# Dilated value slabs and the last down-projection with 512 moving columns, folded sums, and reordered starts and ends, in a three-layer fp32 block on one core

## The chip, the core and the metric

The kernel runs on one core of a Trainium2 chip (trn2). The metric is the device time of one execution in microseconds (us). The core has five instruction streams: PE (matmuls; the profile lists its weight loads apart as PEld), DVE, ACT, POOL (element-wise engines) and SP, which here only issues DMA transfers. They run side by side and meet at semaphores.

## The reference, cut to what matters

Sequence 256, width 1024, everything fp32. A first block has two layers (an even mixer and an odd mixer, each followed by a squared-ReLU MLP) and ends in an RMS norm; a second block has one layer and ends in another.

```python
def first_block(x, ...):                     # x: 1 x 256 x 1024
    for layer in range(2):
        xn = rms_norm(x, norm_mix[layer])
        x = x + (even_mixer if layer == 0 else odd_mixer)(xn, ...)
        x = x + sq_relu_mlp(rms_norm(x, norm_mlp[layer]), w1[layer], w2[layer])
    return rms_norm(x, norm_final)

def odd_mixer(xn, w_in, w_o, cos, sin):      # three dilation groups, 16 heads of 64
    hcat = (xn @ w_in).reshape(b, s, 3, 3, 16, 64)
    q, k = rope(hcat[:, :, :, 0]), rope(hcat[:, :, :, 1])
    v = hcat[:, :, :, 2]
    return dilated_attention(q, k, v) @ w_o

def second_block(x, mem, ...):
    h = rms_norm(x, mix_norm_gain)
    # one projection feeds a linear recurrence, block attention, attention over mem, and gates
    x = x + (sum_of_gated_branches) @ w_out
    h = rms_norm(x, ffn_norm_gain)
    g = causal_dwconv(h @ w_ffn_gate)
    x = x + (gelu(g) * (h @ w_ffn_up)) @ w_ffn_down     # 3072 -> 1024
    return rms_norm(x, final_norm_gain)
```

## The kernel before, in words

**Weights in slabs.** All weights stream from memory in 192 slabs of up to 128 x 2048 values, in the order that `weight_plan` writes out by hand. SP loads slab n into one of five buffers (`raw`). ACT rounds it to a high part (`whi`, one of three buffers, L975), DVE or POOL subtracts to get the low part (`wlo`, L1357 on DVE, L2020 on POOL). `ahead(n)` on each engine prepares slab n+2. A product (`product`, L515) takes three matmuls for each 128 x 128 weight block: high by high, high by low, low by high. The activations are kept feature by row (`XT`, with `XH` and `XL` as its two parts), so that usually the weight block is stationary and 256 tokens move. `tokens` turns this round: 128 tokens are stationary and 256 weight columns move; the dilated values use it.

**Norms.** Squares of `XT` are added up chunk by chunk into `acc(slot)`, 128 x 512 (`add_square`, on DVE or POOL). `sums` then multiplies with ones on PE to add over the partitions: two plain fp32 matmuls of 256 columns, one for each half of `acc`, and where `cols` is set four more of one column. The profile lists each plain fp32 matmul as two.

**Attention.** Units of work run through a software pipeline over steps s. On PE, `attend(first, n, s)` issues the scores of unit s (L648), the transposes of unit s-2 (L656) and the values of unit s-3 (L685). DVE takes maxima (L1425, L1431) and normalises (L1440), ACT does the exponentials (L1037) and copies the transposed probabilities (L1046), or DVE does (L1448). Other work is put between the steps by hand. In the even layer this is among others the memory input: PE transposes it into four banks (`turn_in`, L587), and DVE's `memory_low` (L1623) is what frees a bank. In the odd layer there are 36 slabs of q, k and v: 10 ahead of the first step, the other 26 beside steps 0 to 23. Each q or k slab (24 in all) goes through a rotation: ACT copies it (L1191) and issues four DMAs that swap halves (L1195), POOL multiplies (L2083), DVE adds (`rotate`, L1696). The four values slabs of a head group use `tokens`.

**Second block.** Gates and branches are blended by DVE (L1895, L1897), ACT makes the high part of the merged rows (L1271) and DVE the low part (L1901). Then follow the output projection `OUT2`, the gated feed-forward (`FF`, 24 slabs) and the last down-projection (`FD`, 12 slabs). Its result stays feature by row; squares, gain, transposes back (L940), sums (L958) and the last scaling come behind it.

## Time and profile before

| | |
|---|---|
| median of 3 runs | 1265.96 us (1265.52 to 1267.0) |
| the profiled execution | 1267.13 us, span 1265.3 us |
| PE busy | 1245.1 us, 98% |
| DVE, ACT, POOL busy | 820.8, 618.7, 274.8 us |
| mean granted PE clock | 0.994 |
| DMA | 214 MB, 169 GB/s |

The span goes from the first to the last instruction; the 1.8 us beside it lie outside of what the profile shows. Busy time of PE contains the pipeline latency of a matmul, so rates are better read from long runs of matmuls in the chain than from the mean duration.

### The profile page before, as it was taken

What the parts mean: (1) busy time and instruction counts of PE and PEld (TensorE: products, weight loads), DVE (VectorE), ACT (ScalarE), POOL (GpSimd) and SP (SyncE); (2) the same over time, 40 slices, a digit from 0 to 9 for tenths busy, and PEclk for the clock granted to TensorE, in tenths of its full rate; (3) what the DMA queues carried; (4) which work ended last, traced back from release to release, by engine and by line L of the source; (5) the groups of instructions that cost most, each with busy time, mean ns of one, the idle gap of its engine ahead of it and who ended that gap; (6) DMA issues with size and microseconds to landing.
All of it is one profiled execution on the core that took longest, in us unless ns stands there. A gap on an engine that the chain in (4) does not pass through costs nothing.

```text
span 1265.3 us, 23972 instructions
## 1 busy us (share of the span) xinstructions
PE 1245.1 (98%) x10309; PEld 1207.0 (95%) x10309; DVE 820.8 (65%) x1106; ACT 618.7 (49%) x765; POOL 274.8 (22%) x205
## 2 busy tenths in 40 slices
PE   7999999999999999999999999999999999999997
PEld 7968899999999999999999999999999999999997
DVE  6768666655565666666877655487876477665653
ACT  5565455544344454545555553345665445444441
POOL 2500010000021202020310000389211595444000
PEclk9999999999999999999999999999999999999998
DMA  9543356555576655464355655555553455555550
GB/s 262 185 134 101 106 170 191 177 189 176 191 225 204 188 170 181 150 191 151 101 166 171 196 171 195 170 172 173 170 165 134 163 170 168 187 180 188 179 167 34
DMA packets 194711, 214.00 MB, mean 169 GB/s; under 512 B 5235, under 2 KB 182718, under 8 KB 194606
## 3 DMA queue, kind: packets, MB, share of 16 engines
q1 hardware_dynamic: 189518, 204.93, 50.3%
q10 hardware_dynamic: 4896, 7.08, 2.0%
q8 instruction: 81, 1.33, 0.5%
q0 software_dynamic: 192, 0.46, 0.1%
q14 instruction: 24, 0.20, 0.1%
HBM read 205.11 MB, written 1.05 MB: 163 GB/s over the span
## 4 chain that ended last, share of the span: by engine, by line
PE 92%; DVE 3%; ACT 2%; POOL 1%; DMA 1%; issue 1%; ACTq 0%; SPq 0%; DVEq 0%; POOLq 0%
PE ps L515 79%; PE ps L648 3%; PE ps L551 3%; PE ps L685 2%; PE ps L656 2%; DVE wlo L1357 1%; PE ps L572 1%; PE ps L535 1%; DVE XL L1391 1%; POOL wlo L2020 1%; DMA TB<-TA 0%; ACT whi L975 0%; ACT SN L1037 0%; ACT XH L1007 0%; ACTq L1195 0%
## 5 line engine op out<-in xcount | busy, mean ns | idle before, releaser
L1357 DVE TENSOR_TENSOR wlo<-raw,whi 128x2048 fp32r<-128x2048 f32 (+1 forms) x155 | 360.1, 2326 | 202.1 <-ACT whi L975 202.0
L515 PE MATMUL ps<-XH,whi 128*128 128x256 f32 x1592 | 451.8, 285 | 0.0
L515 PE MATMUL ps<-XH,wlo 128*128 128x256 f32 x1592 | 448.3, 283 | 0.3 <-DVE wlo L1357 0.3
L515 PE MATMUL ps<-XL,whi 128*128 128x256 f32 x1592 | 448.0, 283 | 0.0
L975 ACT ACTIVATE whi<-raw 128x2048 fp32r<-128x2048 f32 (+1 forms) x189 | 359.5, 1905 | 176.6 <-PE ps L515 154.7
L515 PEld LDWEIGHTS ps<-XH,whi 128*128 128x128 f32 x1592 | 304.3, 192 | 3.2 <-issue 2.9
L515 PEld LDWEIGHTS ps<-XH,wlo 128*128 128x128 f32 x1592 | 304.3, 192 | 0.9 <-DVE wlo L1357 0.8
L515 PEld LDWEIGHTS ps<-XL,whi 128*128 128x128 f32 x1592 | 304.3, 192 | 0.0
L2020 POOL TENSOR_TENSOR wlo<-raw,whi 128x512 fp32r<-128x512 f32 x136 | 180.3, 1358 | 319.5 <-ACT whi L975 319.5
L515 PE MATMUL ps<-HH,whi 128*128 128x256 f32 x832 | 229.5, 283 | 0.0
L515 PE MATMUL ps<-HL,whi 128*128 128x256 f32 x832 | 229.3, 283 | 0.0
L515 PE MATMUL ps<-HH,wlo 128*128 128x256 f32 x800 | 226.5, 283 | 1.0 <-POOL wlo L2020 1.0
L515 PEld LDWEIGHTS ps<-HH,whi 128*128 128x128 f32 x832 | 157.5, 192 | 0.0
L515 PEld LDWEIGHTS ps<-HL,whi 128*128 128x128 f32 x832 | 157.5, 192 | 0.0
L515 PEld LDWEIGHTS ps<-HH,wlo 128*128 128x128 f32 x800 | 153.6, 192 | 1.2 <-POOL wlo L2020 1.2
L2083 POOL TENSOR_TENSOR TB<-TB,BIG 128x512 f32<-128x512 f32 x24 | 42.7, 1781 | 367.4 <-DMA TB<-TA 367.4
L1037 ACT ACTIVATE SN<-SN,stat 128x512 f32<-128x512 f32 (+2 forms) x64 | 38.2, 597 | 102.2 <-DVE stat L1425 93.2
L515 PE MATMUL ps<-whi,XH 128*128 128x256 f32 x256 | 73.2, 286 | 0.0
L515 PE MATMUL ps<-whi,XL 128*128 128x256 f32 x256 | 72.4, 283 | 0.0
L515 PE MATMUL ps<-wlo,XH 128*128 128x256 f32 x256 | 72.4, 283 | 0.0
L515 PE MATMUL ps<-OH,whi 128*128 128x256 f32 x192 | 56.3, 293 | 0.0
L1079 ACT ACTIVATE HH<-TB 128x512 fp32r<-128x512 f32 x32 | 20.2, 632 | 72.7 <-DVE TB L1513 72.7
(229 smaller groups left out, 1604.0 us busy)
## 6 DMA issues: line engine op xcount, KB each, us to landing
raw<-in_mlp_w_dram SPq DMA_DIRECT2D x64, 1024.0 KB, 5.4
raw<-in_od_w_in_dram SPq DMA_DIRECT2D x36, 1024.0 KB, 5.4
raw<-in_w_in_dram SPq DMA_DIRECT2D x24, 1024.0 KB, 5.2
raw<-in_w_ffn_gate_dram SPq DMA_DIRECT2D x12, 1024.0 KB, 5.1
raw<-in_w_ffn_up_dram SPq DMA_DIRECT2D x12, 1024.0 KB, 5.1
raw<-in_w_ffn_down_dram SPq DMA_DIRECT2D x12, 1024.0 KB, 5.0
raw<-in_ev_w_in_dram SPq DMA_DIRECT2D x6, 1024.0 KB, 11.6
TB<-TA ACTq DMA_DIRECT2D x96, 64.0 KB, 4.1
```

What stands on the lines that cost most here:

```text
L515: m = pe.matmul(to, l[c][a], r[c][b], start=first and k == 0, stop=last and k == 3 * n - 1)
L535: i = pe.matmul(b[:, m * S:m * S + S], w[m][c][a], x[c][z], start=k == 0, stop=k == len(order) - 1)
L551: i = pe.matmul(b[n][:, m * S:m * S + S], h[a], x[c][z], start=m == c == a == z == 0, stop=m == 1 and c == 7 and z == 1)
L648: m = pe.matmul(banks[u][:, lo:hi], l, r, start=start, stop=stop)
L656: m = pe.transpose(b[:, to:to + P], SN[:, u % 3, of:of + P], ident[:, :])
L685: m = pe.matmul(b[p0:p0 + n, a:z], v, PT[:, u % 3, lo:hi], start=start, stop=stop)
L975: act.activation(whi_of(n), raw_of(n), ACT.Copy, scale=1.0).then_inc(*tell(s_whi, ("whi", n)))
L1037: m = act.activation(SN[:, u % 3, lo:hi], src[:, lo:hi], ACT.Exp, bias=stat[:, u % 3, k:k + 1], scale=-1.0 if biased else 1.0, accum_out=s ...
L1079: act.activation(HH[:, 512 * j:512 * j + 512], TB[j % 2][:, :], ACT.Copy, scale=1.0).then_inc(*tell(s_xhi, ("hhi", layer, j)))
L1357: dve.tensor_tensor(wlo_of(n), raw_of(n), f32(whi_of(n)), ALU.subtract).then_inc(*tell(s_wlo, ("wlo", n)))
L2020: m = pool.tensor_tensor(lo[:, v], r[:, v], f32(hi[:, v]), ALU.subtract)
L2083: pool.tensor_tensor(z, z, twice(RP[:, S:512]), ALU.mult).then_inc(*tell(s_pool, ("sine", k)))
```

## The change

Seven edits in one.

1. The dilated values come in slabs of 4 k-chunks by 512 columns (eight heads), two slabs to a product of 128 tokens by 512 columns. They have half as many matmuls, of 512 columns each. The order of the 36 slabs is the list `DILATED`; 14 stand ahead of the first step and one beside each of steps 0 to 21. The first three output slabs (`pieces`) go one block to each of steps 22 to 33.
2. The last down-projection makes rows instead of features: 128 tokens stationary, 512 weight columns moving. `XT` is transposed to rows during the feed-forward (`rows_in`). Squares, mean and scaling are done on rows; the last gain is loaded spread over all partitions.
3. `sums` gets one folded half: the engine that adds the squares adds the two halves of `acc` too.
4. On PE the values of unit s-3 are issued ahead of the transposes of unit s-2. On DVE `memory_low` is issued ahead of the outputs of the step.
5. In the blend ACT prepares the branch slabs' successors ahead of the high parts of the merged rows.
6. The identity and first gains are loaded from ACT's queue, ahead of which nothing stands, and ACT does one small activation early (its table is loaded then).
7. `keep_busy` puts 12 matmuls of ones between the first transposes.

```diff
-    for hb in range(4):
-        for g, n in ORDER:
-            add("odd", wo, 0, 8, ((3 * g + n) * 16 + 4 * hb) * 64, 256)
+    for kind, b, g, k in DILATED:
+        if kind == "qk":
+            add("odd", wo, 0, 8, ((3 * g + k) * 16 + 4 * b) * 64, 256)
+        else:
+            add("odd", wo, 4 * k * P, 4, ((3 * g + 2) * 16 + 8 * b) * 64, 512)
...
-    down("fd", A["w_ffn_down_2"][0], 24)
+    for half in range(2):
+        for k in range(6):
+            add("fd", A["w_ffn_down_2"][0], 4 * k * P, 4, 512 * half, 512)
...
+    return qk(0) + v(0) + qk(1) + qk(2) + v(1) + qk(3)
...
+EARLY = 14
...
+        pieces = {22 + 4 * k + j: [(k, j)] for k in range(3) for j in range(4)}
...
-            def sums(name, slot, n=2, cols=False, dilated=False):
+            def sums(name, slot, n=1, cols=False, dilated=False):
...
+                if 0 <= s - 3 < n and members(group_of(first + s - 3))[-1] == first + s - 3:
+                    values(group_of(first + s - 3))
                 if 0 <= s - 2 < n:
                     transposes(first + s - 2)
-                if 0 <= s - 3 < n and members(group_of(first + s - 3))[-1] == first + s - 3:
-                    values(group_of(first + s - 3))
...
+            keep_busy(3)
             b = bank(("mixgain",))
...
+            keep_busy(4)
             for c2 in range(4):
+                if c2 == 2:
+                    keep_busy(2)
                 turn_in(("x", c2), [xrow[:, t, :] for t in range(2)], ("x", c2 // 2), c2)
+            keep_busy(3)
...
+                    for t in range(2):
+                        if k == 0:
+                            bank(("odd v", hb, g, t))
+                        b = ps[bank_of.get(("odd v", hb, g, t), 0)]
...
+                        product(b[:, :], xt, w_ready(n, 4, 0, 512), event, first=k == 0, last=k == 1)
...
+                if EARLY + s < len(DILATED):
+                    odd_slab(EARLY + s)
...
+            for q in range(2):
+                b = [bank(("down", 2, q, t)) for t in range(2)]
+                for k in range(6):
...
+                        product(b[t][:, :], ht, w_ready(n, 4, 0, 512), event, first=k == 0, last=k == 5)
...
-            b = bank(("last",))
-            once.wait_ge(*at(("norm", "n7")))
...
-            rows_out(3)
...
                 if s == 14:
+                    ahead(BLENDS + BLEND.index(("branch", 4)))
+                    ahead(BLENDS + BLEND.index(("branch", 5)))
                     branch(4)
                     branch(5)
...
+            for t in range(2):
+                squared_rows(1, t)
+                row_root(t)
+                scaled_row(t, 1)
+            once.wait_ge(*at(("row", 1, 1)))
+            act.dma_start(out[0, P:2 * P, 512:1024], YR[:, 1, 512:1024]).then_inc(*tell(s_out, ("out", 1), by=16))
...
+                if done:
+                    a = acc(slot)
+                    once.wait_ge(*at(("summed", norm, i)))
+                    dve.tensor_tensor(a[:, 0:S], a[:, 0:S], a[:, S:2 * S], ALU.add).then_inc(*tell(s_sum, ("norm", norm)))
...
-                attend(EVEN, 16, s)
+                attend(EVEN, 16, s, lambda: memory_low(s - 6) if 6 <= s < 10 else None)
...
+            for t in range(2):
+                row_sums(1, t)
+                row_mean(t)
+                row_scale(t)
```

On DVE, at steps 6 and 7 of the even layer, the instructions stand so before; OL is the low part of an attention output, HL that of the memory input (L1623 is `memory_low`).

```order
L1425 ISA SN,stat<-ps0,BIG 128x256
L1425 ISA stat 128x1
L1458 TENSOR_TENSOR OL<-ps2,OH 128x256
L1623 SCALAR_TENSOR_TENSOR HL<-ps6,V,HL 128x256 x2
L1437 RECIPROCAL stat<-stat 128x2
L1440 TENSOR_SCALAR SN<-SN,stat 128x256 x2
```

And so after, where L1669 is `memory_low` and L1504 the output:

```order
L1471 ISA SN,stat<-ps0,BIG 128x256
L1471 ISA stat 128x1
L1669 SCALAR_TENSOR_TENSOR HL<-ps6,V,HL 128x256 x2
L1504 TENSOR_TENSOR OL<-ps1,OH 128x256
L1483 RECIPROCAL stat<-stat 128x2
L1486 TENSOR_SCALAR SN<-SN,stat 128x256 x2
```

The instruction that frees bank 6 has moved in front of the output, which waits for ACT.

On ACT, at the end of the blend, before (whi<-raw prepares a weight slab; HH<-BIG is the high part of merged rows):

```order
L1277 ACTIVATE BIG<-BIG 128x2048
L1055 ACTIVATE OH<-ps0 128x256
L975 ACTIVATE whi0<-raw2 128x2048
L1271 ACTIVATE HH<-BIG 128x512 x2
L975 ACTIVATE whi1<-raw3 128x2048
L1271 ACTIVATE HH<-BIG 128x512 x2
L975 ACTIVATE whi2<-raw4 128x2048
```

And after:

```order
L1303 ACTIVATE BIG<-BIG 128x2048
L1082 ACTIVATE OH<-ps0 128x256
L1002 ACTIVATE whi0<-raw2 128x2048
L1002 ACTIVATE whi1<-raw3 128x2048
L1297 ACTIVATE HH<-BIG 128x512 x4
L1002 ACTIVATE whi2<-raw4 128x2048
```

The second output slab (raw3) no longer stands behind the first two merged pieces.

On PE, the end of the program before:

```order
L515 MATMUL ps3<-HH,wlo1 128x256
L515 MATMUL ps3<-HL,whi0 128x256
L940 MATMUL ps4<-ident,BIG 128x128 x4
L958 MATMUL ps5<-ones,SQ 128x1 x4
L940 MATMUL ps6<-ident,BIG 128x128 x4
```

And after:

```order
L535 MATMUL ps1<-wlo1,HH 128x512
L535 MATMUL ps1<-whi0,HH 128x512
L535 MATMUL ps1<-whi0,HL 128x512
L535 MATMUL ps1<-wlo1,HH 128x512
L294 UNCONDITIONAL_BRANCH
```

Nothing is left for PE behind the last product.

## Rows read from the trace of the kernel before

**Rows 1.** The page: busy us, share of the span, instructions.

```profile
PE 1245.1 (98%) x10309; PEld 1207.0 (95%) x10309; DVE 820.8 (65%) x1106; ACT 618.7 (49%) x765; POOL 274.8 (22%) x205
```

**Rows 2.** Whom PE waited for: us in total, times, longest.

```profile
PE ps L587 <- DMA BIG<-in_x_dram: 2.5, 2, 2.1
PE ps L648 <- DVE HL L1623: 2.2, 1, 2.2
PE ps L958 <- DVE SQ L1367: 2.1, 1, 2.1
...
PE ps L515 <- POOL wlo L2020: 1.0, 1, 1.0
```

**Rows 3.** Chain that ended last, by time: start us, us, what.

```profile
24.43 0.86 PE ps L572 x4
25.30 0.79 PE ps L576 x8
...
80.96 1.72 PE ps L791 x4
...
1219.39 17.27 PE ps L515 x144
```

**Rows 4.** Chain in the even layer, from 88 us.

```profile
89.44 4.46 PE ps L648 x16
93.89 1.04 PE ps L656 x4
94.94 1.82 PE ps L685 x8
...
103.53 2.53 PE ps L648 x16
106.06 0.59 PE ps L656 x4
106.65 1.01 PE ps L685 x8
```

**Rows 5.** Timeline of DVE there; in brackets its idle time before.

```profile
88.17 0.42 DVE L1458 TENSOR_TENSOR OL<-ps,OH 128x256 fp32r<-128x256 f32 x1 [2.21 <-ACT OH L1055]
...
90.75 0.68 DVE L1448 COPY PT<-ps 128x512 f32<-128x512 f32 x1
```

**Rows 6.** Windows: busy (instructions) of PE, PEld, DVE, ACT, POOL; PEclk; DMA, GB/s.

```profile
89.70:96.50 6.80, 6.80 (x28) 3.03 (x26) 4.58 (x13) 2.67 (x10) 0.00 (x0) 0.50 0.01 2
...
600.00:624.00 24.00, 24.00 (x238) 21.57 (x233) 21.72 (x55) 16.09 (x32) 10.60 (x8) 1.00 0.29 89
```

**Rows 7.** Timeline: the start, and POOL at the end of the blend.

```profile
1.63 1.84 SPq L2152 DMA_DIRECT2D BIG<-in_x_dram  x4
...
7.14 1.28 ACT L1007 ACT_TABLE_LOAD   x1 [7.14 <-DVE XT L1543]
...
23.02 2.29 DVE L1357 TENSOR_TENSOR wlo<-raw,whi 128x2048 fp32r<-128x2048 f32 x1 [1.18 <-ACT whi L975]
...
1020.84 21.85 POOL L2020 TENSOR_TENSOR wlo<-raw,whi 128x512 fp32r<-128x512 f32 x16 [3.16 <-ACT whi L975]
```

**Rows 8.** Chain through the rotation of one slab.

```profile
416.18 0.61 ACTq L1195
...
417.46 5.64 DMA TB<-TA
...
423.16 2.82 POOL TB L2083
```

**Rows 9.** Timeline of the tail.

```profile
1254.40 0.42 DVE L1493 TENSOR_TENSOR TA<-ps,RS 128x256 f32<-128x256 f32 x1 [2.00 <-PE ps L515]
...
1256.04 0.69 DVE L1367 TENSOR_TENSOR SQ<-SQ 128x512 f32<-128x512 f32 x1 [0.75 <-ACT SQ L991]
...
1260.02 0.71 ACT L1347 ACTIVATE BIG<-BIG,RS 128x512 f32<-128x512 f32 x1
...
1260.76 1.82 SPq L2182 DMA_DIRECT2D out_dram<-BIG  x4
```

More of the change, by code:

```diff
@@ L724, in mlp, with keep_busy @@
                 down(layer, W2[layer], h_ready(layer, 32))
+            def keep_busy(n):
+                once.wait_ge(*at("ones"))
+                for _ in range(n):
+                    pe.matmul(ps[7][:, 0:P], ones[:, :], ones[:, :], start=True, stop=True)
+            keep_busy(3)
             b = bank(("mixgain",))
@@ L930, in tensor, with rows_in @@
             features_by_chunks([FF], x)
-            features(FF + 1, x, between=lambda: sums("n6", 0))
+            features(FF + 1, x, between=lambda: sums("n6", 0, cols=True))
+            def rows_in(j):
+                b = bank(("rows", j))
+                for t in range(2):
+                    for c in range(2):
+                        m = pe.transpose(b[:, t * S + c * P:t * S + c * P + P], XT[:, 2 * j + c, t * P:(t + 1) * P], ident[:, :])
+                m.then_inc(*tell(s_product, ("product", "rows", j)))
@@ L1318, in scalar @@
                 if j == 0:
-                    root("n6", 0)
+                    root("n6", 0, cols=True)
                 else:
@@ L1322, in scalar @@
                 ahead(FF + 2 * j + 1)
+                if j in (3, 5, 7, 9):
+                    i = (j - 3) // 2
+                    b = take(("rows", i))
+                    act.activation(XR[:, :, 256 * i:256 * i + 256], pair(b[:, :]), ACT.Copy, scale=1.0).then_inc(
+                        *tell(s_act_out, ("taken", "rows", i)))
                 once.wait_ge(*at(("ffn conv", j)))
@@ L1325, in scalar @@
             ffn_high(11)
-            def rows_out(j):
-                b = take(("rows", j))
-                act.activation(orow[:, :, 256 * j:256 * j + 256], pair(b[:, :]), ACT.Copy, scale=1.0).then_inc(
-                    *tell(s_act_out, ("taken", "rows", j)))
-            for j in range(4):
-                for s in range(3):
-                    ahead(FD + 3 * j + s)
-                once.wait_ge(*at(("xt", "down", 2, j)))
-                if j == 0:
-                    once.wait_ge(*at("ones"))
-                    act.activation(GG[:, 0:1], ones[:, 0:1], ACT.Sqrt)
-                square("n7", 1, j, x0[j], ("xt", "down", 2, j))
-                if j:
-                    rows_out(j - 1)
@@ L1342, in scalar, with squared_rows @@
[L1342 to L1347 removed]
+            def squared_rows(q, t):
+                once.wait_ge(*at(("xr", q, t)))
+                act.activation(SQ[:, 2 * q + t, :] if q + t < 2 else SN[:, 2, :], XR[:, t, 512 * q:512 * q + 512], ACT.Square, accum_out=stat[:, t, q:q + 1]).then_inc(
+                    *tell(s_square, ("rows squared", q, t)))
@@ new lines, in row_root, with scaled_row @@
+            def row_root(t):
+                once.wait_ge(*at(("mean", "n7", t)))
+                act.activation(r7[:, t:t + 1], r7[:, t:t + 1], ACT.Sqrt).then_inc(*tell(s_root, ("sqrt", "n7", t)))
+            def scaled_row(t, q):
+                once.wait_ge(*at(("root", "n7", t)))
+                once.wait_ge(*at(("yr", q, t)))
+                v = YR[:, t, 512 * q:512 * q + 512]
+                act.activation(v, v, ACT.Copy, scale=r7[:, t:t + 1]).then_inc(*tell(s_act, ("row", t, q)))
@@ L1988, in vector @@
             ffn_low(11)
-            for j in range(4):
-                down(2, FD, 3, r6, j)
-                if j:
-                    add_square("n7", 1, j, j == 3)
-                for c in (2 * j, 2 * j + 1):
-                    m = dve.tensor_scalar(XG[:, c, :], XT[:, c, :], gain("fin2", c), None, ALU.mult)
-                m.then_inc(*tell(s_dve, ("gained", j)))
-            b = take(("last",))
-            r7 = RS[:, 1, 0:2]
-            dve.tensor_scalar(r7, b[:, 0:2], 1.0 / D, EPS, ALU.mult, ALU.add).then_inc(
-                *tell(s_dve_out, ("mean", "n7"), ("taken", "last")))
@@ new lines, in vector @@
+            for k in range(6):
+                ahead(FD + k)
+            for t in range(2):
+                row_sums(0, t)
+            for t in range(2):
+                once.wait_ge(*at(("rows squared", 0, t)))
+                m = dve.tensor_scalar(stat[:, t, 2:3], stat[:, t, 0:1], 1.0 / D, EPS, ALU.mult, ALU.add)
+            m.then_inc(*tell(s_dve, "rows' first half"))
+            for k in range(6, 12):
+                ahead(FD + k)
+            once.wait_ge(*at("rows' first half"))
```

242 lines of the change are left out of this document (119 added, 123 removed).

## The prediction

> **What bounds the kernel now.** I read four views, in this order. The page first: PE is busy for 1245.1 of 1265.3 us, no other engine for more than 65% [rows 1]. That busy share holds pipeline latency, so the next view is the list of PE's waits: few of its entries reach 1 us: the start (2.5), the even layer (2.2), the tail (2.1) and the blend (1.0) [rows 2]. Everywhere else PE goes from one product into the next. The chain of what ended last shows the pace: 144 matmuls in 17.27 us, 119.9 ns each [rows 3]. Last come the windows, where one stretch of the even layer runs at a granted clock of 0.50, 1.2 GHz, while the other one is at 1.00, 2.4 GHz [rows 6]. So three things shorten this kernel: less matmul time, the few waits, and the tail behind the last product. Work taken off another engine counts only where one of these waits hangs on it.
>
> **512 moving columns.** The dilated values had 12 slabs of 48 matmuls, 576 in all, and the last down-projection had 12 x 48 too. Both become half as many, of 512 columns: 1152 matmuls of 256 turn into 576 of 512. One of 256 costs 119.9 ns [rows 3]. At 2.4 GHz and one column a cycle, 256 columns take 106.7 ns, so 13.2 ns are something else. What is it? No fp32r matmul of 512 columns is in the trace. Plain fp32 ones are, at two cycles a column: of 256 columns 215 ns (0.86 over 4), where the columns take 213.3, and of 512 columns 430 ns (1.72 over 4), where they take 426.7 [rows 3]. Their remainder is 2 to 3 ns. With a single moving column one still costs 99 ns (0.79 over 8) [rows 3]: that is about what loading a 128 x 128 weight block takes. So where the columns last 213 ns the load hides, and where they last 107 ns it nearly fills the time. I read the 13.2 ns as the load that does not quite hide. With 512 columns it would have 213 ns to hide in, and a matmul would cost 213.3 + 2.5 = 215.8, say 216 ns. The saving is 2 x 119.9 - 216 = 23.8 ns, times 576 = 13.7 us. The bounds: if the 13.2 ns are paid once by each matmul whatever its length, it costs 226.5 ns and the saving is 7.7 us; if the pace goes with the columns alone (0.468 ns a column), nothing is saved. A loss would need a remainder above 26 ns, twice that of 256 columns. I take 13.7, since plain fp32 is the nearest row and its remainder did not grow.
>
> The Trainium skill ("TensorE: Matmul & The Clock Gate", section "Back-to-back issue gap") has the isolated gap as N/2.4 + 2.5 ns, 109.2 at 256 columns and 215.8 at 512. The trace disagrees at 256 (119.9 ns), so by that formula alone, at both ends, the edit would be worth 1.5 us, and with the measured 256 it would be worth 13.8.
>
> **Folded sums.** Eight of the ten `sums` lose one plain matmul of 256 columns, two instructions of 215 ns, 0.43 us each and 3.4 together. Five with `cols` also lose four instructions of 99 ns, 0.39 us each and 2.0 together; n6 gets as many new ones, 0.4. Net 5.0 us, all of it PE time between products. The fold is one more 256-wide addition, on DVE about half of 0.69 us [rows 9], on POOL half to all of 1.37 (21.85 over 16) [rows 7]. PE's waits name no `sums` except the last, L958 [rows 2], so it stays covered by the products ahead; uncovered it would cost 0.4 to 1.4 us at one norm.
>
> **Even layer.** PE stands 2.2 us before the scores at 89.44 [rows 2], because `memory_low` frees the bank only behind the output at 88.17, for which DVE itself stood idle for 2.21 us waiting for ACT [rows 5]. `memory_low` now goes into that idle time and PE starts at 87.24. What is late next is the values, now ahead of the transposes: they want the copy that DVE makes at 90.75 for 0.68 us [rows 5], which moves up by the 0.85 that `memory_low` takes behind the output (88.59 to 89.44) [rows 4, 5], to end near 90.6. PE's scores end at 87.24 + 2.53 = 89.8 [rows 4], so 0.8 us of the wait come back: 1.4 gained. The second part is the clock. It fell at 89.70, just behind the 2.2 us of idleness, and stayed for 6.8 us [rows 6]. In it scores, transposes and values took 4.46 + 1.04 + 1.82 = 7.32 us; the same at full clock take 2.53 + 0.59 + 1.01 = 4.13 [rows 4]. That is 3.2 more, if the clock stays up. I take 4.6 in all, and for the lower end that the clock falls all the same: then the values and transposes still take 2.86, PE is through at 87.24 + 2.53 + 0.8 + 2.86 = 93.4 instead of 96.8, and the slow time left until 96.5 costs half of itself, 1.5, on what follows: 1.8. Nothing is added above 4.6.
>
> **Blend.** PE waits 1.0 us for POOL's low part of the second output slab [rows 2]. POOL had been idle for 3.16 us until ACT's high part came [rows 7], which stood behind two merged pieces. Now it goes first. The merged pieces come later by one preparation of a slab, and PE wants the first of them only behind branch 5. I take 1.0 and bound it by 0 and 1.3. Steps 13 and 14 gain nothing else, as PE runs through them.
>
> **Start.** The table load of 1.28 us stood between the first `XT` and everything that followed [rows 7], and x is asked for at 1.63, behind two small loads that take some 0.9 us to issue [rows 7]. Both leave the path: 2.2 us at most until PE's first product. From there to the third slab DVE's low part decides (23.02, after 1.18 idle for ACT) [rows 7]; it moves by what ACT gains less what its raw slabs, whose loads move by 0.9 only, hold back. I take 1.7, bounds 0.5 and 2.8. `keep_busy` costs nothing while it fits into the gaps: four matmuls, eight instructions of 0.11 to 0.22 us (half of 215 ns, and twice that at the lower clock), are 0.9 to 1.7 us in a wait of 2.1 [rows 2].
>
> **Tail and rows.** From the last product (1254.4) to the end are 10.9 us now, through DVE, ACT, DVE, PE, ACT and DVE in turn. After, it is one DVE addition (0.69), a square with its sum (0.71 and about 0.2), mean, root and reciprocal (about 0.2 each), one scaling (0.71) [rows 9], some eight hand-overs of 0.05, and a transfer: issue 0.45 (1.82 over 4) and the 2.7 that now lie between the last issue and the end. Together 6.4, so 4.5 are saved, bounds 3.5 and 5.5. Twelve of the sixteen transposes lay between products already; the other four now do too and add 0.4.
>
> **Dilated stage.** The moved slabs add nothing by themselves. Two more steps at the end have only one output block beside them; there DVE is at 21.72 of 24 us while PE still does not wait [rows 6], and a step's content is as before. I count nothing.
>
> **The sum.** 13.7 + 5.0 + 4.6 + 1.0 + 1.7 + 4.5 - 0.4 = 30.1 us. Against the profiled execution's 1267.1 (a span of 1265.3 and 1.8 around it) that is 1237.0; the median of the runs lies 1.2 lower, at 1266.0, so 1235.9.
>
> **The rivals.**
> *Fixed cost (0.20).* The 13.2 ns belong to each matmul. For it: the 256-column pace never varies. Against it: plain fp32 pays 2 to 3 [rows 3]. 1235.9 + 6.0 = 1242.
> *The clock or the bank still bites (0.12).* The even layer gives 1.8 instead of 4.6, and the start little, since its slabs wait for memory. For it: attention without a slab beside it remains between 82 and 92 us. 1240.
> *The dilated stage starves (0.06).* Twelve q and k slabs stand in a row, ten of them beside the steps. One rotation is a copy and a last addition of 0.7 each (as the 512-wide ones of [rows 9]), four issues of 0.61, 5.64 for the DMA and 2.82 on POOL, 12.3 us [rows 8, 9], and two are in flight. Two steps of PE are 14.7: 48 matmuls of 119.9 ns are 5.75, and attention is some 1.6, for 24 us hold about eight steps with 12 matmuls beside each [rows 6]. Queueing that eats the 2.4 between them and some more costs around 8 us: 1244.
> *Pace by columns (0.04).* Nothing from 512: 1250.
> *Slower (0.02).* The same rotation chain as a bound: 16 slabs beside steps are 8 pairs, and from 14.7 + 3.8 = 18.5 us a pair on, the 30 us are eaten; at 19 it is 1271. Against it: this needs a landing of some 12 us instead of 5.64.
> *Short stream (0.01).* Each matmul of 512 columns at far less than its columns' time. At 131 ns it would be 576 x 85 = 49 us better than in the main case, 1187. Against it: 430 ns for 512 columns at two cycles each [rows 3] leave no column skipped. The Trainium skill has such a figure in the same section (about 131 ns a matmul at 512 columns in a sustained stream); the trace disagrees already at 256 columns, where 119.9 ns lie above the 98 on the line between its two figures (81 at 128 columns, 131 at 512).
>
> **How the numbers follow.** The main case keeps 0.55 and gives 1236, by itself 1231 to 1240: the start and tail at their good ends and the last small waits gone give some 4 to 5 less, a half-gained clock 3 more. The fixed cost and the clock reach to 1242 and, together with a smaller start, 1245. Below 1230 and above 1245 I leave about 0.15. A measurement of this kernel can tell about 0.2%, 2.5 us, from no change. Everything but the slower case is faster by more than that: faster 0.95, same 0.02, slower 0.03.
>
> **What would show it.** In the profile after: 576 matmuls of 128x512 fp32r at 216 ns from start to start (24 in 5.2 us) and 226 under the rival; L572's heir at 22 instructions; no wait of PE at `memory_low` and a clock of 1.00 from 89 to 97 us; no wait for POOL's low part; no L958; about 6.4 us behind the last matmul. The prediction is wrong if the wide matmuls come at 240 ns, or if the list of PE's waits names `QKV` operands, TB or transposed probabilities with several us.

## The result: 12.2 us faster, not 30.1

The changed kernel takes 1254.3 us (median, 1252.3 to 1255.0), the kernel before 1266.5 beside it: a ratio of 0.9901, 95% interval 0.9883 to 0.9918. It is faster, and it lies outside the range of 1230 to 1245. The profiled execution has a span of 1253.1 us against 1265.3.

The page of the profile after (busy us, share, instructions) answers to [rows 1]:

```profile
PE 1230.1 (98%) x9717; PEld 1174.4 (94%) x9717; DVE 817.3 (65%) x1093; ACT 620.8 (50%) x772; POOL 270.9 (22%) x208
```

Whom PE waited for, after (us in total, times, longest), answers to [rows 2]:

```profile
PE ps L535 <- POOL wlo L2079: 3.7, 2, 2.6
PE ps L668 <- DVE BIG L1739: 3.0, 1, 3.0
PE ps L676 <- DVE SN L1486: 1.9, 1, 1.9
PE ps L757 <- DMA TA<-in_norm_mix_dram: 1.8, 1, 1.8
PE ps L535 <- DVE wlo L1399: 1.7, 2, 1.2
PE ps L705 <- DVE PT L1494: 1.5, 2, 1.3
...
PE ps L668 <- DVE HL L1669: 0.4, 1, 0.4
```

Two of the waits that the prediction spoke of are nearly gone: `memory_low` (last line) went from 2.2 to 0.4, and L958 no longer exists. The one for POOL's low part in the blend grew from 1.0 to 2.6 us, and there are new ones: a rotation's result (L1739 writes `QKV`), the normalised probabilities SN (L1486), and their transposes PT. The prediction had named `QKV` operands and transposed probabilities as signs of its own failure; SN it had not.

To see where the time went I took the time from one matmul's start to the next and split it into the median of its kind and the excess over that. What counts as a kind moves some 5 us between the first row and the rows up to 100 us and from 1250 (by line and shape alone the first row is 1221.0 and 1209.4); the rows from 100 to 1250 hardly depend on it. Sums in us of the profiled executions:

| | before | after |
|---|---|---|
| all matmuls at their kind's median pace | 1216.0 | 1204.9 |
| excess 0 to 75 us (start, norms) | 8.8 | 8.2 |
| excess 75 to 100 (even layer) | 6.9 | 3.4 |
| excess 100 to 575 | 11.0 | 8.4 |
| excess 575 to 600 (end of the dilated slabs) | 1.1 | 9.9 |
| excess 600 to 1250 | 9.2 | 11.0 |
| excess in the tail, from 1250 | 3.2 | 0 |

PE has about 11 us less to do, where the prediction had 18.3 (13.7 + 5.0 - 0.4). Of the 9.9 us gained in waits (even layer, tail, attention, start) 8.8 are lost again in one place, 575 to 600 us, and 1.8 behind it. The other 1.8 us of the span's difference lie before the first row: PE's first instruction, now a matmul on ones, starts at 1.04 us instead of 2.83.

### The profile page after: what moved, and what is told of

It reads as the page before. It is cut to its first block, busy times and chain, and to the rows that moved or that the text cites. A ratio compares the mean times of both kernels' runs of the same rounds, so it can differ in the third digit from the quotient of the medians.

```text
span 1253.1 us, 22776 instructions
## 1 busy us (share of the span) xinstructions
PE 1230.1 (98%) x9717; PEld 1174.4 (94%) x9717; DVE 817.3 (65%) x1093; ACT 620.8 (50%) x772; POOL 270.9 (22%) x208
## 4 chain that ended last, share of the span: by engine, by line
PE 80%; DVE 4%; ACT 3%; POOL 2%; issue 2%; DMA 1%; ACTq 0%; DVEq 0%; POOLq 0%
PE ps L535 72%; PE ps L705 2%; PE ps L668 2%; PE ps L571 2%; PE ps L676 2%; ACT whi L1002 1%; DMA TB<-TA 1%; POOL wlo L2079 1%; DVE wlo L1399 1%; DVE XL L1437 1%; POOL TB L2145 1%; ACTq L1228 0%; DVE SN L1471 0%; ACT XH L1034 0%; DVE XT L1529 0%
## 5 line engine op out<-in xcount | busy, mean ns | idle before, releaser
L535 PE MATMUL ps<-HL,whi 128*128 128x256 f32 x640 | 175.0, 283 | 0.0
L535 PE MATMUL ps<-HH,whi 128*128 128x256 f32 x640 | 175.0, 283 | 0.0
L535 PE MATMUL ps<-HH,wlo 128*128 128x256 f32 x608 | 172.2, 283 | 2.6 <-POOL wlo L2079 2.6
L2145 POOL TENSOR_TENSOR TB<-TB,BIG 128x512 f32<-128x512 f32 x24 | 38.4, 1598 | 384.0 <-DMA TB<-TA 384.0
L535 PEld LDWEIGHTS ps<-HL,whi 128*128 128x128 f32 x640 | 120.7, 192 | 0.1
L535 PEld LDWEIGHTS ps<-HH,whi 128*128 128x128 f32 x640 | 120.7, 192 | 0.0
L535 PEld LDWEIGHTS ps<-HH,wlo 128*128 128x128 f32 x608 | 116.7, 192 | 2.8 <-POOL wlo L2079 2.8
L535 PE MATMUL ps<-wlo,XH 128*128 128x512 f32 (+1 forms) x160 | 55.7, 348 | 1.2 <-DVE wlo L1399 1.2
L535 PE MATMUL ps<-whi,XH 128*128 128x512 f32 (+1 forms) x160 | 56.3, 352 | 0.0
L535 PE MATMUL ps<-whi,XL 128*128 128x512 f32 (+1 forms) x160 | 55.5, 347 | 0.0
```

The costliest lines, as they stand in the source:

```text
L535: m = pe.matmul(to, l[c][a], r[c][b], start=first and k == 0, stop=last and k == 3 * n - 1)
L2145: pool.tensor_tensor(z, z, twice(RP[:, S:512]), ALU.mult).then_inc(*tell(s_pool, ("sine", k)))
```

## The experiments

Each kernel ran in turn with the kernel before, which took 1266.5 to 1266.8; the changed kernel's 1254.3 is the comparison. The 95% interval of a ratio is about 0.0015 to either side for four runs, 1.9 us, so two experiments that lie less than some 2 us apart are not told apart by their times. There a comparison of two profiles helps, in which the same instruction of PE is looked up in both and its start compared.

One such comparison bears on everything below. `e2_probe`, `e5_branch_old` and `e5_woven` have the changed kernel's instructions up to 1000 us, and yet they do not pass the end of the dilated slabs alike. The windows of that place (columns as in [rows 6]), for the changed kernel and these three, are:

```profile
575.00:600.00 25.00, 19.44 (x158) 17.91 (x158) 16.04 (x36) 10.54 (x19) 5.06 (x5) 0.86 0.30 93
575.00:600.00 25.00, 20.78 (x189) 18.96 (x189) 17.88 (x41) 11.99 (x23) 7.60 (x6) 0.93 0.36 113
575.00:600.00 25.00, 20.64 (x178) 18.75 (x178) 16.58 (x40) 10.67 (x20) 5.87 (x5) 0.86 0.31 95
575.00:600.00 25.00, 21.53 (x197) 19.88 (x197) 19.28 (x41) 11.98 (x23) 7.57 (x6) 0.93 0.40 127
```

PE waits there 5.6, 4.2, 4.4 and 3.5 us in all, the clock is at half for 6.8, 3.4, 6.8 and 3.4 us, and from 580 to 600 us the three gain 2.6, 1.4 and 3.6 us on the changed kernel's profile with the same code. So the excess of 9.9 in the table is the worst of four executions, and what the stage lost is 5 to 9 us. An experiment whose time moves by 1 to 4 us may owe it to this place.

### What a matmul of 512 columns costs

`e1_split` is the change with

```diff
-m = pe.matmul(b[:, :], l[c][a], r[c][z], ...)
+for e0, e1 in zip(edge, edge[1:]):
+    m = pe.matmul(b[:, e0:e1], l[c][a], r[c][z][:, e0:e1], ...)
```

> The changed kernel, with every matmul of 512 moving columns done as two on the same stationary block: 256 + 256 in the dilated values and in the second half of the last down-projection, 384 + 128 in its first half. Slabs, loads, waits and copies stay. Theory A (about 13 ns are paid by each matmul whatever its length): a pair of 256 takes 240 ns from start to start and 384 + 128 takes 173 + 67 = 240, against 227 for one of 512 now; 576 more matmuls cost 7.5 us: 1261.8. Theory B (my prediction's: a weight load that does not quite hide behind 107 ns of columns): a 128-column matmul cannot be shorter than the load of about 99 ns, so 384 + 128 takes about 160 + 99 = 259 ns, and 256 + 256 takes 240. Theory C (a repeated stationary block is not paid twice): pairs at 227, no change in time.

Measured: 1266.1, 11.8 us slower, where theory A had 7.5. `e2_probe` puts the pace by itself behind the last product:

```diff
+for rows, cols, n, same in (...):
+    for i in range(24):
+        pe.matmul(spare[0:cols, 0:n], H(0 if same else i, rows, cols), W(i, n, rows), start=True, stop=True)
```

> The changed kernel with 216 more fp32r matmuls behind its last product, 24 of each kind, into a spare bank (the output does not use them): stationary 128x128 with 512, 384, 256 and 128 moving columns and a new block each time, 128x128 with 256 columns and always the same block, stationary 128x64 and 128x96 with 256 columns, stationary 64x128 with 256, and 128x64 with 512. Theory A (13.2 ns for each matmul with a full 128x128 block, independent of the columns): 226.5, 173.2, 119.9, 66.6 ns. Theory B (a load of about 99 ns that has to hide): 216 to 227, 173 or less, 119.9, then about 99 to 112 at 128 columns. For the partial blocks, attention's rows have 108 ns at 256 columns and a 64-wide block: I expect 108 for 128x64 and 64x128, and 227 minus 12 = 215 for 128x64 with 512; 128x96 lies between if the cost goes with the block. The span grows by some 30 us of probe.

Windows of the probe, each from the first start of one kind to the first of the next, so that its length over 24 is the pace (the last one ends at the last start, so there it is over 23; length, PE, PEld busy (instructions), PEclk, DMA share, GB/s); 512, 384, 256 and 128 columns, then 256 with the same block, block 128x64, 128x96 and 64x128 at 256, and 128x64 at 512:

```profile
1244.83:1250.27 5.44, 5.43 (x24) 4.50 (x24) 1.00 0.52 193
1250.27:1254.46 4.19, 4.19 (x25) 4.17 (x24) 1.00 0.00 0
1254.46:1257.33 2.87, 2.87 (x25) 2.87 (x25) 1.00 0.00 0
1257.33:1259.96 2.63, 2.63 (x26) 2.63 (x25) 1.00 0.02 6
1259.96:1262.88 2.92, 2.92 (x26) 2.92 (x26) 1.00 0.00 0
1262.88:1265.62 2.74, 2.74 (x26) 2.74 (x25) 1.00 0.00 0
1265.62:1268.49 2.87, 2.87 (x26) 2.72 (x24) 1.00 0.00 0
1268.49:1271.55 3.06, 3.06 (x25) 2.92 (x24) 1.00 0.00 0
1271.55:1276.90 5.35, 5.35 (x24) 3.15 (x24) 1.00 0.00 0
```

That is 227, 175, 120 and 110 ns. From 256 columns on, each matmul costs its columns and some 13 ns (213.3 + 13.3, 106.7 + 13.3): theory A. At 128 it does not fall to 67 but stays at 110, the floor that theory B had put at 99 to 112 and ascribed to the load. The kernel that split the matmuls fits in sum. Its pairs of 384 + 128 come three in 0.86 us, in this piece of its PE timeline (a row holds two matmuls):

```profile
1200.23 0.45 PE L547 MATMUL ps<-whi,HL 128*128 128x384 f32 x2
1200.52 0.45 PE L547 MATMUL ps<-wlo,HH 128*128 128x384 f32 x2
1200.81 0.45 PE L547 MATMUL ps<-whi,HH 128*128 128x384 f32 x2
1201.09 0.45 PE L547 MATMUL ps<-whi,HL 128*128 128x384 f32 x2
```

That is 287 ns a pair (the probe's paces make 175 + 110 = 285), where the pair of 256 takes 240 and theory B had 259. Start by start it is 226 behind a 384 and 60 behind a 128, so only the sum agrees. The same block in every matmul saves nothing (122 ns), so theory C falls. What the 13 ns are is not shown. By the starts of its own 24, a block of 64 columns comes at 114 and one of 96 at 116 (its window also holds the 0.2 us to the next kind), one of 64 rows at 120 in the median, and 64 columns with 512 moving at 233; I had expected 108 for the first and third and 215 for the last. The split costs 144 x 60 + 432 x 13 = 14.3 us of PE; 11.8 show. Its profile has 5.5 us of excess between 575 and 600 instead of 9.9; that the slower value slabs caused this is not shown, since the same code varies by up to 3.6 there. In the changed kernel itself the wide matmuls start 227 ns apart:

```profile
1199.88 0.39 PE L535 MATMUL ps<-wlo,HH 128*128 128x512 f32 x1
1200.11 0.39 PE L535 MATMUL ps<-whi,HH 128*128 128x512 f32 x1
1200.33 0.39 PE L535 MATMUL ps<-whi,HL 128*128 128x512 f32 x1
1200.56 0.39 PE L535 MATMUL ps<-wlo,HH 128*128 128x512 f32 x1
```

The Trainium skill ("TensorE: Matmul & The Clock Gate", section "Back-to-back issue gap") has the isolated gap as N/2.4 + 2.5 ns, 215.8 at 512 columns. The trace disagrees here too: 226.7.

### The start

`e4_no_keep` takes the matmuls on ones away:

```diff
-keep_busy(3)
 b = bank(("mixgain",))
...
-keep_busy(4)
...
-    if c2 == 2:
-        keep_busy(2)
...
-keep_busy(3)
```

> The changed kernel without its 12 matmuls on ones at the start. Theory A (four of them stand between the gain rows, which land at 4.46 now instead of 2.83, and the transposes of x, and so delay them from about 5.2 to 6.53): the transposes start 1.0 to 1.9 us earlier and PE's first product too; but DVE's low part of the third slab is held by its own chain, so 0.5 to 1.3 us of the time: 1253.0 to 1253.8. Theory B (x lands at 6.5 anyway): nothing moves. Theory C (without them the clock is at 1.2 GHz for longer): the first products take twice the time until it rises, 1 to 3 us slower.

Measured: 1251.9 (ratio 0.9881), 2.4 us faster. PE after the change, and then without them (start us, us; idle before in brackets):

```profile
4.46 0.28 PE L757 MATMUL ps<-ident,TA 16*128 16x16 f32 x1 [1.77 <-DMA TA<-in_norm_mix_dram]
4.67 2.08 PE L751 MATMUL ps<-ones 128*128 128x128 f32 x8
6.53 1.92 PE L607 MATMUL ps<-ident,BIG 128*128 128x128 f32 x8
```

```profile
4.36 0.28 PE L756 MATMUL ps<-ident,TA 16*128 16x16 f32 x1 [4.36 <-DMA TA<-in_norm_mix_dram]
4.68 1.97 PE L607 MATMUL ps<-ident,BIG 128*128 128x128 f32 x8
```

Theory A. The gain rows landed at 2.83 before, and now, issued at the same 1.16 us but from ACT's queue beside x, at 4.4. x is there by then, but eight instructions on ones stand ahead of its transposes: 1.85 us. Without the filler the first products came at half the later pace until 12.8 us (eight in 1.88 us from 9.81, later eight in 0.96), with it at nearly full pace from 11.37; the slow products cost less than what the filler took. How much it took is read from the first norm's sums (L592), where PE arrived at 24.27 before, at 23.91 with the change and at 22.71 without the filler: 1.2 us, inside theory A's range. The rest of the 2.4 appears at 580 to 600 us, in code that this edit does not touch.

### The even layer

`e6_memory_old`:

```diff
-attend(EVEN, 16, s, lambda: memory_low(s - 6) if 6 <= s < 10 else None)
+attend(EVEN, 16, s)
+if 6 <= s < 10: memory_low(s - 6)
```

> The changed kernel with DVE's low part of the memory at its old place, behind the whole attention step instead of inside it. Theory A (my prediction's: this placement is what removed the wait of 2.2 us before the scores and with it the fall of the clock, 4.6 us in all): the wait of some 2 us at 87 to 89 comes back, the clock falls for 6.8 us behind it, 3.5 to 4.6 us slower: 1257.8 to 1259. Theory B (the order of values and transposes, and the start, kept the clock up): the wait comes back and the clock stays, 1255.5 to 1256.

Measured: 1259.9, 5.5 us slower. PE waits 3.00 us before those scores, and the window behind them shows the clock at half again (columns as in [rows 6]):

```profile
90.60:97.50 6.90, 6.90 (x32) 4.18 (x29) 3.82 (x10) 2.03 (x7) 0.00 (x0) 0.51 0.00 0
```

Theory A. The profiles agree: the same instruction behind this window starts 5.7 us later than in the changed kernel. The wait that comes back (3.00, and 0.97 more for HL at 99) is longer than the 2.2 of the kernel before, and the table gives 3.5 for what the stage gained. The prediction's term of 4.6 lies between the two. `e9_values_last` puts transposes ahead of values again on PE:

```diff
-values(...)
 transposes(first + s - 2)
+values(...)
```

> The changed kernel with PE's old order inside a step of attention: transposes, then values, on PE alone. Theory A (values first want the copy of the probabilities one place earlier, which is the wait of 1.31 us for DVE's copy at 90.8, and they cost nothing elsewhere): the wait at 90.8 falls to under 0.5, PE waits 0.5 to 1 us for SN or the copy at other steps instead; 0 to 1.5 us better, 1252.8 to 1254.3. Theory B (values first is what lets PE run through the dilated steps, whose excess over the bare pace fell by 1.9 us between 400 and 575): 2 to 4 us slower, 1256 to 1258.

Measured: 1254.7. The wait at 90 is 0.38 instead of 1.31, and 2.26 us for SN are left at 586 instead of three waits of 5.6 together; excess comes back between 450 and 575 (1.5 us). In time the order makes no difference that shows: theory B, 2 to 4 us slower, falls.

### Folded sums

`e10_unfolded` sets `n=2` in `sums` and drops the folds on DVE and POOL.

> The changed kernel with the sums over the partitions unfolded: two matmuls a norm again, two for each column pair, and no folding addition on DVE or POOL (the last layer's sum keeps its columns, which the rows need). PE has 8 x 0.43 + 6 x 0.39 = 5.8 us more. Theory A (my prediction's: the folds cost nothing elsewhere): 5.8 us slower, 1260.1. Theory B (what PE saves at a norm it then waits for: 1.16 us for DVE's low part at 26.35 and 1.07 for POOL's at 836 come from it): both waits shrink by what the sums there take (0.8 to 1.3 each), so 3.5 to 4 us slower: 1257.8 to 1258.3.

Measured: 1255.8, only 1.5 us slower, less than both theories. PE's matmuls take 6.1 us more at the median pace. Three waits of the changed kernel, which are not in this trace, give 2.8 back: 1.16 for DVE's low part at 26.35, 0.57 at 643, 1.07 for POOL's at 836. The rest lies in the dilated stage (excess 575 to 600: 5.7 instead of 9.9), where the same code varies nearly as much; that any of it follows from the folds is not shown. Theory B's 3.5 to 4 us is therefore not refuted.

### The blend

`e5_branch_old` restores ACT's order at the last two branches, `e5_woven` tries a third:

```diff
 ahead(BLENDS + BLEND.index(("branch", 4)))
+merged(0)
 ahead(BLENDS + BLEND.index(("branch", 5)))
+merged(1)
+ahead(OUT2)
-branch(4)
-branch(5)
+merged(2)
+merged(3)
```

> The changed kernel with ACT's order of the last two branches as before: preparation, pieces 0 and 1, preparation, pieces 2 and 3. Theory A (my prediction's, 1.0 us for the edit): 1.0 us slower, 1255.3, with a wait of 1 us or more for the second output slab at 1023. Theory B (what the edit took from the second output slab it gave to the third, 2.58 us instead of 1.01): the wait for the second slab is back, now with PE 5 us earlier 1 to 2 us, and that for the third falls to under 1 us; the same within 1 us, 1253.5 to 1255.

Measured: 1252.3, 2.0 us faster than the change, at the edge of what times can tell. PE waits 1.01 for the second output slab and 0.3 later, and not at all for the third. From the same instruction at 1007 us to the last one this profile takes 1.0 us less than the changed kernel's: theory B, the same within 1 us. The other 1.7 us of its profile's lead were there before, in the same code.

> The changed kernel with ACT's four merged pieces woven between its preparations at step 14: preparation of branch 4's turn, piece 0, preparation of branch 5's turn, piece 1, preparation of the first output slab's turn, pieces 2 and 3. Now both branch preparations stand first, and the second waits 3.57 us for PE to give up a buffer with piece 0 queued behind it (it could start at 1009.3 and starts at 1010.9), and the next preparation stands behind all four pieces, at 1021.9, though its buffer is free from about 1015. Theory A (this order is why POOL's low part is late for the third output slab): PE's wait of 2.58 us at 1029 goes, no other above 0.5 takes its place, 2.5 us better, 1251.8, and more where the clock fell behind it. Theory B (POOL at 1.3 us for each quarter cannot keep up there once PE comes 5 us earlier): the wait stays above 1.5 us.

Measured: 1251.2 (ratio 0.9874), 3.1 us faster; the wait is gone: theory A. From 1007 us to the last matmul its profile takes 2.9 us less than the changed kernel's. ACT after the change, from its timeline:

```profile
1009.10 1.91 ACT L1002 ACTIVATE whi<-raw 128x2048 fp32r<-128x2048 f32 x1 [3.57 <-PE ps L535]
1010.92 0.62 ACT L1297 ACTIVATE HH<-BIG 128x512 fp32r<-128x512 f32 x1
1015.19 0.63 ACT L1297 ACTIVATE HH<-BIG 128x512 fp32r<-128x512 f32 x1 [3.65 <-DVE BIG L1936]
1018.60 0.63 ACT L1297 ACTIVATE HH<-BIG 128x512 fp32r<-128x512 f32 x1 [2.78 <-DVE BIG L1936]
1021.39 0.63 ACT L1297 ACTIVATE HH<-BIG 128x512 fp32r<-128x512 f32 x1 [2.16 <-DVE BIG L1936]
1021.92 1.90 ACT L1002 ACTIVATE whi<-raw 128x2048 fp32r<-128x2048 f32 x1
```

The preparation that moved ahead waits 3.57 us for PE to give up its buffer, with the first merged piece behind it; the next one stands behind all four pieces, and PE waits until 1029 for the low part that POOL makes from it. Woven, ACT's preparations stand at 1005.86, 1010.93 and 1017.35, and POOL runs without a pause (`x16` in one row):

```profile
1001.75 24.18 POOL L2077 TENSOR_TENSOR wlo<-raw,whi 128x512 fp32r<-128x512 f32 x16 [1.86 <-ACT whi L1002]
```

### The end of the dilated slabs

In the changed kernel PE's waits there and DVE's timeline (in brackets idle time) are:

```profile
584.76 0.66 PE L676 MATMUL ps<-ident,SN 128*128 128x128 f32 x4 [1.86 <-DVE SN L1486]
589.88 1.15 PE L668 MATMUL ps<-BIG 64*128 64x256 f32 x12 [3.02 <-DVE BIG L1739]
591.71 0.70 PE L705 MATMUL ps<-PT,BIG 128*64 128x128 f32 x4 [0.69 <-ACT PT L1073]
```

```profile
579.86 2.44 DVE L1399 TENSOR_TENSOR wlo<-raw,whi 128x2048 fp32r<-128x2048 f32 x1 [1.56 <-ACT whi L1002]
582.22 0.68 DVE L1757 TENSOR_TENSOR BIG<-ps,BIG 128x512 f32<-128x512 f32 x1
582.82 0.68 DVE L1739 TENSOR_TENSOR BIG<-BIG,TB 128x512 f32<-128x512 f32 x1
583.42 0.68 DVE L1471 CUSTOM_DVE_ANT_0 SN<-ps,BIG 128x512 f32<-128x512 f32 x1
...
588.93 0.69 DVE L1739 TENSOR_TENSOR BIG<-BIG,TB 128x512 f32<-128x512 f32 x1 [3.00 <-POOL TB L2145]
```

Two things happen behind the last slab (step 21). DVE's softmax stands behind a low part, a product's copy and a rotation's addition, 3.8 us of work that a slab of 5.75 us on PE covers and a block of 1.44 us does not. And the last rotation, begun at 579.66, ends at 589.6, 10 us, with only steps 22 and 23 in between; before, the last slabs were two value slabs, both beside step 22 (step 23 had none). The clock falls behind it, as a window shows:

```profile
591.00:597.80 6.80, 6.11 (x38) 5.79 (x37) 5.00 (x14) 4.41 (x8) 0.32 (x1) 0.50 0.00 0
```

The waits are 5.6 us, and 6.8 us at half clock cost up to 3.4: together about the 8.8 of the table. In the three other profiles of this code the waits are 4.2, 4.4 and 3.5. Five kernels go at it:

```diff
-EARLY = 14
+EARLY = 16          # e3; e7: also pieces from step 20; e8: also rotate() two steps later
-    return qk(0) + v(0) + qk(1) + qk(2) + v(1) + qk(3)
+    return qk(0) + v(0) + qk(1) + qk(2) + qk(3)[:2] + v(1) + qk(3)[2:]
```

> The changed kernel with 16 slabs instead of 14 ahead of the dilated steps, and two of the last six q/k slabs ahead of the second value slabs (they may not come earlier, since the second values write over those of the first eight heads). The last q/k slab then stands beside step 19 instead of 21, so its rotation (12.3 us from copy to last addition) has steps 20 to 23 to hide behind instead of 22 and 23. Theory A (the latency of the last rotations at the end of the row of q/k slabs makes PE stand 1.9 + 3.0 + 0.7 us at 585 to 592 and brings the clock down for 6.9 us behind it): waits of under 1 us there, the clock stays at 1.00, 8 us less: about 1246. Theory B (the rotations starve throughout, two steps of PE being shorter than one rotation's queue): the wait only moves ahead by two steps and the time stays within 2 us of 1254. Theory C (a step without a slab is bound by the softmax on DVE and ACT): as many us come back as waits for transposed probabilities or SN in the later steps, 1250 to 1254.

Measured: 1256.9; waits of 2.81 for SN and 2.41 for probabilities, at 581 and 587, where steps 20 and 21 are bare. That is theory C's mechanism, though its range ended at 1254; A falls. Part of the time is not of this place: its profile has 6.8 us at half clock from 1028 us too, behind the unchanged wait in the blend.

> As the run with 16 slabs ahead of the steps, and the twelve blocks of the output projection begin at step 20 instead of 22 (each step until 31 has one), so that no step between the last slab and the first block is without a product beside it. The run with 16 ahead left steps 20 and 21 bare and PE stood there 2.8 us for SN and 2.4 for transposed probabilities. Theory A (what PE lacks at this place is matmul work beside the steps that the last rotations and the DVE's backlog need): the waits at 581 and 587 fall to under 1.5 us together and the clock stays up, 6 to 8 us better than that run's 1256.9: about 1249 to 1251; steps 32 and 33 are bare now and may cost 1 us. Theory B (DVE's own work in a step without a slab is longer than PE's, whatever stands beside it): the same 5 us of waits, 1255 to 1257.

Measured: 1257.2; 1.41 and 2.43 at the same places and 2.79 in the bare steps at 622. Theory B.

> The same with 15 slabs ahead, one of the last six q/k slabs ahead of the second value slabs, and the output blocks from step 21. The last rotation has steps 21 to 23 to hide behind, three instead of two. Theory A: one step more is some 3 us of PE more in front of the scores of step 24, so that the 3.0 us for the rotation's result go, while the 1.9 for SN behind the last slab stay: 1250 to 1252. Theory B: unchanged, 1254.

Measured: 1255.9; 2.35 and 1.08. The wait for the rotation went, one for the probabilities took its place: neither theory's number.

> As the run with 15 slabs ahead and the output blocks from step 21, and DVE's last addition of the last rotation stands behind its part of step 23 instead of step 21 (the scores that need it are those of step 24). Theory A (the wait in DVE's own queue is what costs: the addition waits for the DMA and POOL, and the softmax of the next head is queued behind it, so PE waits for transposed probabilities and SN; in the run with 16 ahead DVE stood idle 1.80 us at 582.2 before that addition): the two waits at 583 and 589 (2.35 and 1.08) fall to under 1 us together, the clock stays up, 3 to 5 us better than that run's 1255.9: 1251 to 1253. Theory B (what is late is DVE's work as such, and the waits are PE catching up with it): unchanged within 1 us.

Measured: 1253.7, 2.2 less than its pair; but the 2.35 us at 585 stayed, and there DVE is never idle: that part is DVE's turn as such, theory B. Of the other wait 0.60 is left.

> As the run with 16 slabs ahead and the output blocks from step 20, with the last rotation's addition behind step 22 instead of step 20, and the blocks spread: steps 24, 29 and 34 have none, instead of 32 to 34, where that run had PE stand 2.79 us at 622. Theory A: all three waits (1.41, 2.43, 2.79) go to under 1 us each and the clock stays at 1.00, 1248 to 1251. Theory B as in the other run: within 1 us of 1257.

Measured: 1253.2, 4.0 less than its pair; waits of 1.42, 0.82, 0.37 and 0.63, the clock at 1.00 there. A and B each hold for a part. Only this last one, of the five, is below 1254.3 by as much as 1 us, so none is shown to be faster than the change.

### Put together

`c2_start_woven` is the change with the edits of e4 and e5_woven.

> The changed kernel without the matmuls on ones at the start and with the woven pieces in the blend; the dilated stage as in the change. By itself the one gave 2.4 us and the other 3.1. If they add up: 1248.8. If the clock's falls behind the dilated waits decide as much as the waits: 1247 to 1251.

Measured: 1248.1, ratio 0.9856, 6.2 us less than the change, where the two gave 5.5 by themselves: they add up within the scatter.

> The same, with 16 slabs ahead, the late last addition and the spread output blocks, which alone gave 1.1 us: 1247.7 if all add up; with no wait over 1.5 us left in the program the clock should not fall, and then 1245 to 1246.

Measured: 1248.6. The clock never falls before the last matmul in its profile, yet nothing is gained over c2, so a clock that stays up does not bring the forecast 1245 to 1246: 1.64 us for SN and small waits at bare steps remain.

> The same again, with two output blocks beside step 20, the first without a slab, and steps 25, 28, 31 and 34 without any. PE has 1.44 us more to do at the place where it waits 1.42 us for SN. Theory A (it is the want of work beside the first step without a slab, while DVE is a whole slab's turn behind): the wait goes below 0.3 and nothing takes its place, 1.4 us better than the run before it and more if the clock stays. Theory B (DVE's turn is late anyway, and the blocks add 1.07 us of it each): the wait moves to step 21 or 22 at the same size.

Measured: 1250.6. The wait for SN fell to 0.98, and others came up behind it, 2.06 the largest, at 614: nearer theory B.

`c4_values_end` is c2 with another slab standing last (and its output blocks spread):

```diff
-EARLY = 14
+EARLY = 17
-    return qk(0) + v(0) + qk(1) + qk(2) + v(1) + qk(3)
+    return qk(0) + v(0) + qk(1) + qk(2) + qk(3) + v(1)
```

> The best version so far (no matmuls on ones at the start, woven pieces in the blend: 1248.1) with another order in the dilated stage: 17 slabs ahead, all of the last q/k slabs ahead of the second value slabs, so that the six value slabs, for which DVE has no product copy and no rotation, stand beside steps 13 to 18 and the last rotation is long over when the slabs end; the twelve output blocks stand in steps 19 to 33, with 22, 26, 30 and 34 bare. Theory A (the waits at the end of the slabs come from slabs with a rotation standing last, when DVE is a whole turn behind): waits of PE between 575 and 600 under 1 us together, the clock stays, 2 to 3 us better: 1245 to 1246; the four bare steps may take back 1. Theory B (the first steps without a slab expose DVE's turn whatever stood before): 1.5 to 2.5 us of waits there as in the other runs, 1248.

Measured: 1247.6, ratio 0.9849 (0.9834 to 0.9863), the lowest of all. The same window as above, here:

```profile
575.00:600.00 25.00, 24.57 (x237) 21.94 (x236) 20.18 (x52) 14.93 (x31) 7.20 (x6) 1.00 0.28 86
```

No wait over 0.3 us and a full clock there: theory A for this place. In each of the 18 other profiles of the changed kernel and its variants PE waits 2.0 us or more there in all, so this is outside of what the same code varies by. What it won it partly paid elsewhere, 1.96 us for probabilities at 613 beside a bare step and 1.79 at 25, and the clock fell for 3.4 us at 26 and again at 91. So over c2 only 0.5 us show, within the scatter. Its four runs took 1248.9, 1249.0, 1246.3 and 1245.9 us at a mean granted clock of 0.997, 0.996, 0.999 and 0.999, so that the runs in which the clock stayed up lie in the forecast 1245 to 1246 or close to it.

> The same best version with PE's old order in a step of attention (transposes, then values). By itself that order was 0.4 us slower than the change, within its spread, with the wait at 90 falling from 1.31 to 0.38 and one wait of 2.26 us at 586 instead of three of 5.6 together. If the order only shifts the phase: 1247.5 to 1249. If the smaller waits also keep the clock from falling at 90 and 586, as it did in the version without it: 1245 to 1246.5.

Measured: 1249.3. Waits at 585 and 589 (1.63, 1.57) stay, where c2 has one of 2.04: the order inside PE's step does not remove them. The clock did not fall before the last matmul, and still the time is not the 1245 to 1246.5 forecast for that.

## Why the prediction was wrong

- **512 columns: 7.5 us, not 13.7.** The failed step is "I take 13.7, since plain fp32 is the nearest row and its remainder did not grow". The remainder belongs to each fp32r matmul; 576 x (239.8 - 226.7) = 7.5. The rival was priced rightly (7.7) and given 0.20. The row with a single column, which I read as the load, fits the floor of 110 ns at 128 columns, but hiding it is not what the 13 ns are: at 512 columns they are still there. What they are stays open.
- **Dilated stage: minus 5 to 9, not 0** (8.8 in the profile of the change, 1.4 to 3.6 less in three others of the same code). "The moved slabs add nothing by themselves" failed. The rival named the place and nearly the price (8 us), but reckoned the throughput of rotations in a row (12.3 us against the 14.7 of two steps of PE). No wait in the middle of the row shows that as a bound, so the rival's price was near by luck; PE waited for the latency of the last one and for DVE's turn behind the last slab. I had compared a step's content and not what stands at the end of the row.
- **Folded sums: 5.0 counted as saved on PE, 2.8 of it waited away;** undone, only 1.5 us show, and why not more is open. "PE's waits name no `sums` except the last" is true and does not say that the next operand has slack. DVE's and POOL's low parts had been just in time.
- **Blend: minus 1.0 to 1.6, not plus 1.0** (1.0 by the profile of the old order, 1.6 by the wait, 2.58 against 1.01). Moving one preparation ahead put a merged piece behind its wait for a buffer and left the next preparation last. "The merged pieces come later by one preparation" counted 1.9 us and not the 3.57 of waiting.
- **Start: 0.4 to the first norm, not 1.7;** without the filler it is 1.6, so the filler took what the rest gained. "`keep_busy` costs nothing while it fits into the gaps" took the gap from the trace of before; the change moved the landing of the rows and with it the gap.
- **Even layer: right,** 4.6 forecast, 3.5 in the table, 5.5 by undoing it; the clock stayed at 1.00 from 86 to 97 us, as forecast.
- **Tail: right,** from 10.9 to 5.9 us, 5.0 for the 4.5 forecast.

The terms of the failed steps do not add up to the 17.9 us missing to the digit, since one profile each was read and the stages depend on each other. The largest are the dilated stage and the 512 columns.

## What to carry to other kernels

When PE is nearly always busy, a gain on PE arrives only as far as the next operand's slack goes: for each place where PE gets faster, read how long before its use the next operand is ready. Where a stage ends, look at its last element: its latency and the helper engine's backlog lose their cover there, so let the elements with the least work behind them stand last. Before a few us are put down to an edit, look in a second profile of the same code whether that place repeats. An instruction moved ahead on an in-order engine brings its own wait with it, and the wait counts, not its duration.

## What the hardware showed that I had not expected

An fp32r matmul with a 128x128 block costs 227, 175, 120 and 110 ns for 512, 384, 256 and 128 moving columns, and repeating the block changes nothing (122). Splitting 512 into 384 + 128 costs 60 ns, into 256 + 256 only 13. The granted clock fell for 3.4 or 6.8 us behind waits of 1.3 to 3 us, but not behind every one. Behind the same waits of 0.45 and 1.3 us at 86 to 91 us it fell in four of sixteen profiles (e8_late_rotate15, e8_late_rotate16, c2_start_woven, c4_values_end) and stayed up in the others, the changed kernel's among them. Behind the wait of 2.6 us near 1027 it fell in nine of twelve, for 6.8 us in two of these, and not in the changed kernel's. What decides between them stays open. Two small loads issued at 0.7 and 1.16 us in both kernels were there for PE at 2.83 when they stood ahead of x in SP's queue, and at 4.4 when they went from ACT's queue beside it.
